# Head norms of two features in one pass of the array, roots in pairs, and the steps of a sparse-attention mixer set around them

## The reference, cut to what matters

```python
def rms_norm(x, g):
    y = xf * lax.rsqrt(jnp.mean(xf * xf, axis=-1, keepdims=True) + EPS)
...
q = rms_norm(q.reshape(B, S, DSA_HEADS, HEAD_DIM), q_g)          # 12 heads: six features of 2 heads
k = rms_norm(k, k_g)
dots = jnp.einsum('bqhd,bsd->bqhs', qib, ki) * IDX_DIM ** -0.5   # the indexer
score = jnp.einsum('bqh,bqhs->bqs', wib, jax.nn.relu(dots))
_, sel = lax.top_k(score, topk)                                  # 128 of up to 512
logits = jnp.einsum('bqhd,bqkd->bqhk', qb, k_sel) * HEAD_DIM ** -0.5 + bias
o = jnp.einsum('bqhk,bqkc->bqhc', softmax(logits), v_sel)
# beside it, with rms_norm on its queries and keys too:
xo = memory_cross_attention(xq, mk, mv, xq_g, xk_g)
```

## Time and profile before

| | |
|---|---|
| median of 3 runs | 1434.66 us (1433.44 to 1435.72) |
| the profiled execution: its own time | 1435.65 us |
| its span on the profile | 1433.8 us |
| PE busy | 1385.7 us (97%) |
| DVE busy | 591.8 us (41%) |
| ACT busy | 328.8 us (23%) |
| POOL busy | 98.2 us (7%) |
| chain that ended last | PE 69%, DMA 12%, SP's queue 8%, DVE 7%, ACT 2% |

### The profile page before, as it was taken

The page is one execution under the profiler, slowest core; times in us unless marked ns, Lnnn a source line. Parts: engine busy times, 40 slices in busy tenths (PEclk is TensorE's granted clock), DMA queues, the critical chain, the costliest instruction groups (busy, mean ns, idle before and its releaser), DMA issues.

```text
span 1433.8 us, 16567 instructions
## 1 busy us (share of the span) xinstructions
PE 1385.7 (97%) x6433; PEld 620.5 (43%) x6433; DVE 591.8 (41%) x1110; ACT 328.8 (23%) x650; POOL 98.2 (7%) x191
## 2 busy tenths in 40 slices
PE   7999999999999999999999989999999999999997
PEld 4464466433333333333354555564343333333332
DVE  4655104434333333333439974244343333333333
ACT  4455102111110110011326774221111111100111
POOL 1001000200000000000000223002000000000000
PEclk9999999999999999999999999999999999999999
DMA  8207394999999999999930030789999999999995
GB/s 284 114 0 231 105 364 174 359 422 428 426 426 427 426 426 428 427 423 421 364 101 1 1 122 1 249 337 357 422 428 426 427 427 427 426 429 424 424 421 232
DMA packets 73999, 457.26 MB, mean 319 GB/s; under 512 B 15884, under 2 KB 23628, under 8 KB 43848
## 3 DMA queue, kind: packets, MB, share of 16 engines
q1 hardware_dynamic: 68160, 447.97, 76.8%
q0 software_dynamic: 4928, 8.22, 1.5%
q10 hardware_dynamic: 840, 0.06, 0.0%
HBM read 457.41 MB, written 10.53 MB: 326 GB/s over the span
## 4 chain that ended last, share of the span: by engine, by line
PE 69%; DMA 12%; SPq 8%; DVE 7%; ACT 2%; issue 1%; POOL 0%; DVEq 0%; ACTq 0%
PE ps L1661 21%; PE ps L1274 18%; PE ps L1679 10%; DMA arena<-in_moe_w_up 8%; PE ps L1697 7%; SPq L587 5%; DMA arena<-in_moe_w_down 4%; SPq L591 3%; PE ps L1688 2%; DVE mix L1997 2%; PE ps L1650 1%; DVE small L1996 1%; PE ps L1576 1%; PE ps L1283 1%; PE ps L1535 1%
## 5 line engine op out<-in xcount | busy, mean ns | idle before, releaser
L1661 PE MATMUL ps<-arena,xT 128*64 128x512 f32 x2048 | 455.0, 596 | 14.5 <-issue 9.8
L1661 PEld LDWEIGHTS ps<-arena,xT 128*64 128x64 f32 x2048 | 150.1, 137 | 299.1 <-issue 291.9
L2335 DVE TENSOR_TENSOR x<-ps,x 128x1024 f32<-128x1024 f32 x120 | 146.5, 1224 | 204.4 <-PE ps L1697 202.1
L1679 PE MATMUL ps<-arena,xT 128*64 128x512 f32 x896 | 199.1, 596 | 2.2 <-ACT xT L1207 1.6
L1274 PE MATMUL ps<-xT,arena 128*128 128x512 f32 x384 | 169.0, 595 | 1.7 <-ACT xT L953 1.3
L1697 PE MATMUL ps<-mix,xT 128*128 128x512 bf16 x720 | 165.8, 380 | 0.0
L1697 PEld LDWEIGHTS ps<-mix,xT 128*128 128x128 bf16 x720 | 65.5, 98 | 119.5 <-issue 48.7
L1679 PEld LDWEIGHTS ps<-arena,xT 128*64 128x64 f32 x896 | 61.8, 137 | 118.4 <-issue 111.4
L1274 PEld LDWEIGHTS ps<-xT,arena 128*128 128x128 f32 x384 | 71.9, 190 | 91.4 <-issue 88.9
L1207 ACT ACTIVATE xT<-ps 128x512 f32<-128x512 f32 x32 | 19.1, 597 | 391.7 <-PE ps L1669 391.7
L1274 PE MATMUL ps<-arena,mix 128*128 128x512 f32 (+1 forms) x256 | 105.6, 568 | 0.0
(11 more groups left out here) (282 smaller groups left out, 1181.7 us busy)
## 6 DMA issues: line engine op xcount, KB each, us to landing
arena<-in_moe_w_gate SPq DMA_DIRECT2D x48, 2048.0 KB, 27.6
arena<-in_moe_w_up SPq DMA_DIRECT2D x48, 2048.0 KB, 26.4
arena<-in_moe_w_down SPq DMA_DIRECT2D x48, 2048.0 KB, 30.4
arena<-in_moe_w_down SPq DMA_DIRECT2D x32, 1024.0 KB, 20.7
arena<-in_moe_w_gate SPq DMA_DIRECT2D x32, 1024.0 KB, 21.3
arena<-in_moe_w_up SPq DMA_DIRECT2D x32, 1024.0 KB, 21.3
arena<-in_w_out SPq DMA_DIRECT2D x4, 2048.0 KB, 11.5
arena<-in_dsa_w_in SPq DMA_DIRECT2D x1, 5120.0 KB, 15.8
```

What stands on the lines that cost most here:

```text
L1661: ins = pe.matmul(ps[e * CAP:(e + 1) * CAP, bank, :], tokT[:, k, e * CAP:(e + 1) * CAP], rows_in[u][:, k, :], start=k == 0, stop=k == KD - 1)
L1679: ins = pe.matmul(ps[e * CAP:(e + 1) * CAP, BANK_Y + c, :], hT[:, j, e * CAP:(e + 1) * CAP], rows_down[u][:, j, c * 512:(c + 1) * 512], st ...
L2335: dve.tensor_tensor(x[:, t, :], ps[:, b:b + 2, :].rearrange("p a n -> p (a n)"), x[:, t, :], ALU.add).then_inc(s_, 1)
```

## The change

`norm_sum_two` takes the place of `norm_sum` for four pairs of features: `xq.0` with `xq.1` in the first mixer, `q.0` with `q.1`, `q.2` with `q.3`, `q.4` with `q.5` in the second. For each it issues four matmuls of 64 x 64 weights, one for each quarter of the array: the first feature's heads on the diagonal, the second's off it. The second feature's sums so lie in its bank with the two heads swapped (`turned`), and ACT reads that bank in two instructions of 64 partitions (`on_bank`). ACT takes Ln of both features and then Exp of both. The sums of `q.0`, `q.2` and `q.4` move behind the next feature's, the square of `q.4` behind the roots of `q.2` and `q.3`, and DVE's rounds and norms are set around them.

```diff
@@ plan(): the banks in PE's order, and who empties them @@
+            for name, last in zip(projections(), ("k", "xq.0", "xq.1")):
                 j.add(f"1.{name}", "act")
+                sums(last)
+            j.add("1.q.1", "act")
+            x_logits(0)
+            x_logits(1)
+            j.add("1.q.2", "act")
+            sums("q.0", "q.1")
...
+        turned = ["0.xq.1", "1.q.1", "1.q.3", "1.q.5"]
@@ ACT @@
+            def on_bank(dst, key, **how):
+
+                b = bank(key[0] + ".sq" + key[1:])
+                if key in turned:
+                    act.activation(dst[0:HD], b[HD:P], bias=eps[HD:P, 0:1], **how)
+                    return act.activation(dst[HD:P], b[0:HD], bias=eps[0:HD, 0:1], **how)
+                return act.activation(dst, b, bias=eps[:, 0:1], **how)
...
                     feature("q.1")
-                    roots("1.q.0")
                     x_exp(0)
                     x_exp(1)
                     feature("q.2")
-                    roots("1.q.1")
+                    root_logs("1.q.0")
+                    root_logs("1.q.1")
+                    root_exps("1.q.0")
+                    root_exps("1.q.1")
                     x_copy(0)
                     x_exp(2)
                     feature("q.3")
-                    roots("1.q.2")
                     x_copy(1)
                     x_exp(3)
                     values(0)
                     values(1)
-                    feature("q.4")
+                    raw(1, "q.4", qT[:, 4, :])
                     x_copy(2)
                     values(2)
                     values(3)
                     l_exps(0)
-                    roots("1.q.3")
+                    root_logs("1.q.2")
+                    root_logs("1.q.3")
+                    root_exps("1.q.2")
+                    root_exps("1.q.3")
+                    squares("1.q.4", qT[:, 4, :], ["1.q.4"])
                     feature("q.5")
@@ PE @@
+            def norm_sum_two(one, two):
+
+                pe.wait_ge(sq_ready, feats[two])
+                lo, hi = slice(0, HD), slice(HD, P)
+                halves = ((lo, lo, one), (hi, hi, one), (lo, hi, two), (hi, lo, two))
+                b = {key: open_bank(key[0] + ".sq" + key[1:]) for key in (one, two)}
+                for n, (r, c, key) in enumerate(halves):
+                    ins = pe.matmul(b[key][c, :], ones_head[r, r], sqb[int(key[0])][r, feats[key] % 2, :], start=True, stop=True)
+                    if n % 2:
+                        ins.then_inc(filled, 1)
...
-                            norm_sum(f"0.xq.{c}")
+                            if c == 0:
+                                norm_sum_two("0.xq.0", "0.xq.1")
...
                     project("q.1", C_Q + P)
-                    norm_sum("1.q.0")
                     x_logits(0)
                     x_logits(1)
                     project("q.2", C_Q + 2 * P)
-                    norm_sum("1.q.1")
+                    norm_sum_two("1.q.0", "1.q.1")
                     x_turn(0)
                     x_logits(2)
                     project("q.3", C_Q + 3 * P)
-                    norm_sum("1.q.2")
...
-                    norm_sum("1.q.3")
+                    norm_sum_two("1.q.2", "1.q.3")
                     project("q.5", C_Q + 5 * P)
                     x_turn(3)
                     x_value(2)
-                    norm_sum("1.q.4")
-                    norm_sum("1.q.5")
+                    norm_sum_two("1.q.4", "1.q.5")
@@ DVE @@
                     x_largest(1)
-                    normalise_q(0)
+                    take_largest(2, 10, 11)
                     x_inverse(0)
-                    take_largest(2, 10, 11)
+                    take_largest(2, 11, 12)
                     x_inverse(1)
-                    take_largest(2, 11, 16)
+                    take_largest(2, 12, 16)
                     x_copy(0)
                     x_largest(2)
+                    normalise_q(0)
                     normalise_q(1)
-                    take_largest(3, 0, 1)
                     x_inverse(2)
-                    take_largest(3, 1, 5)
+                    take_largest(3, 0, 5)
                     x_copy(1)
                     x_largest(3)
                     x_out(0)
-                    normalise_q(2)
+                    take_largest(3, 5, 6)
                     x_inverse(3)
-                    take_largest(3, 5, 9)
+                    take_largest(3, 6, 9)
...
+                    normalise_q(2)
                     normalise_q(3)
```

More of the change, by code:

```diff
@@ L224, in plan, with sums @@
             j.add("1.vT", "act")
-            last = "k"
-            for name in projections():
+            def sums(*names):
+                for name in names:
+                    j.add(f"1.sq.{name}", "act")
+            for name, last in zip(projections(), ("k", "xq.0", "xq.1")):
                 j.add(f"1.{name}", "act")
[L228 to L251, removed]
+                sums(last)
[4 more added lines that the diff above has]
+            sums("q.0", "q.1")
+            x_turn(0)
+            x_logits(2)
+            j.add("1.q.3", "act")
+            x_turn(1)
+            x_logits(3)
+            j.add("1.xo.0", "dve")
+            values(0)
+            values(1)
+            j.add("1.q.4", "act")
+            x_turn(2)
+            j.add("1.xo.1", "dve")
+            logits(0)
+            values(2)
+            values(3)
+            sums("q.2", "q.3")
+            j.add("1.q.5", "act")
+            x_turn(3)
+            j.add("1.xo.2", "dve")
+            sums("q.4", "q.5")
             logits(1)
@@ L910, in root_logs @@
                     act.wait_ge(feat_normed, n - 2)
-                act.activation(rs_view(key), bank(jn), ACT.Ln, bias=eps[:, 0:1], scale=1.0 / HD).then_inc(emptied["act"], 1)
+                on_bank(rs_view(key), key, func=ACT.Ln, scale=1.0 / HD).then_inc(emptied["act"], 1)
             def root_exps(key):
@@ L926, in roots @@
                         act.wait_ge(feat_normed, n - 2)
-                    act.activation(rs_view(key), bank(jn), ACT.Sqrt, bias=eps[:, 0:1], scale=1.0 / HD).then_inc(emptied["act"], 1)
+                    on_bank(rs_view(key), key, func=ACT.Sqrt, scale=1.0 / HD).then_inc(emptied["act"], 1)
             for L in range(2):
```

## The result

| | before | after |
|---|---|---|
| median, us (lowest to highest, 13 runs each) | 1434.66 (1431.44 to 1436.15) | 1436.74 (1435.62 to 1440.19) |
| the profiled execution: own time, span | 1435.65, 1433.8 | 1436.13, 1434.3 |
| PE, DVE, ACT busy, us | 1385.7, 591.8, 328.8 | 1381.5, 591.9, 326.1 |

The ratio of the times is 1.0021 [1.0013, 1.0029]: the change costs 2.1 us by the medians, 3.0 us by the means. The forecast was 1436.6. PE is busy 4.2 us less and the program takes longer. It fell three times in the profile before and twice in this one; e9, the kernel after once more, has four falls and PE busy for 1384.0 us, 2.5 us more. Ratios leave out three executions far from all others: one of e12 (3722.64 us) and two of the kernel before beside the experiments (5122.54 and 1469.49 us).

A forecast was written before the change was run, and what follows sets the result against it. PE and DVE were taken to run side by side, with DVE late at `q.4` and ACT taking over from `q.5`'s sums. 1434.66 + 1.1 (chain) + 0.7 + 0.2 (clock) = 1436.6 us; range 1432.5 to 1438.6.

The forecast's parts named there:

- The price of a double sum: On PE, all four quarters overlap: 0.86 us, or 1.04 us with two changes of shape.
- The third rival: Quarters of a double sum don't overlap: 1437.4 us with corners only, about 1441 us with none; chance 0.07.
- The 3.44 us: Time of a double sum on PE if no quarters overlap, as the prediction read the skill's page.
- The first mixer: PE saves 0.68 us but waits for DVE's norm of `memK`: 0.00 us gained, wait from 2.0 to 2.7 us.
- `q.4`: Second mixer: DVE stands 0.8 us for an Exp, so `q.4` starts 0.28 us later and PE waits 2.0 us.
- The saving passes through: Rival: DVE is in time, ACT's third Ln is covered, PE's -1.9 us reaches the end; 1432.8 us, chance 0.17.
- ACT to `l_exps(1)`: Second mixer: ACT runs without gaps, with half reads and three Ln; `l_exps(1)` comes 1.1 us later.
- PE's last saving hidden behind ACT: Second mixer, sums of `q.4` and `q.5`: PE's -0.78 us is hidden because ACT sets the pace.
- The clock: After the new 2.0 us wait ahead of `q.4`, the granted clock falls in 2/5 of cases: 0.7 us.
- The second rival: The clock falls every time, after the new `q.4` wait and the longer first-mixer wait; 1438.5 us, chance 0.16.
- The first mixer's clock: The longer PE wait in the first mixer can raise its own share of clock falls: 0.2 us.

The follow-up runs named there:

- e9: The kernel after once more, unaltered, timed beside e10, e11 and e12; ratio to before 1.0024.
- e12: e8 without the two extra matmuls in the first mixer; 1432.47 us beside 1434.45 for the kernel before, ratio 0.9991.
- e3: The kernel after with one DVE selection round put between the two norms and `x_inverse(2)`; ratio to before 1.0018.
- e4: The kernel after with one DVE round of the third block moved from ahead of `x_copy(1)` to behind the first group's reciprocal; ratio to before 1.0015.
- e2: The kernel after with each swapped bank read by ACT in one instruction, heads left swapped (wrong roots); ratio to before 1.0008.
- e1: The kernel after with its order kept but the second mixer's sums made singly, without packing; ratio to before 1.0020.
- e8: The kernel after with the e3 and e4 moves, single sums for `xq`, `q.4`, `q.5`, and two extra matmuls in the first mixer; 1432.39 us, ratio to before 0.9988.
- e11: The kernel after with only two repeated matmuls filling PE's first-mixer wait, ahead of `gate.0`; ratio to before 1.0013.
- e6: The kernel after with repeated matmuls filling two PE waits: two in the first mixer, three ahead of `q.4`; ratio to before 1.0008.
- e5: The kernel before with only the first mixer's sums of `xq.0` and `xq.1` packed; ratio to before 1.0003.
- e7: The kernel before with only two repeated matmuls filling PE's first-mixer wait, ahead of `gate.0`; ratio to before 0.9991.
- e10: The kernel after with only three repeated matmuls filling PE's wait ahead of `q.4`; ratio to before 1.0019.

## Why the prediction was right, step by step

The time, the range and the sign held: 1436.74 for 1436.6. ACT's stretch came out 0.5 us dearer than forecast and the fall at `q.4`, priced at 0.7, wasn't seen; that the total is met to 0.1 us is luck.

- **The price of a double sum.** Right: 1.02 us for 1.04. All four quarters start within 0.04 us of each other, and their second records 0.5 us later, in step as the corners of the block gates do. The third rival is dead. The Trainium skill ("TensorEngine Tiling (Array Packing)", Restrictions and Gotchas) says that different row tiles cannot access one PSUM bank simultaneously; the trace disagrees: both row halves write each of the two banks, and start within 0.04 us. The 3.44 us that the prediction drew from this sentence doesn't follow from it, since it says nothing of products in different banks.
- **The first mixer.** `x_logits(0)` unmoved behind a longer wait: right; the wait is 2.49 us, not 2.7. What it does to the clock is below.
- **`q.4`.** Right in mechanism and nearly in size: DVE stood 0.86 us (0.8), `q.4` came 0.36 us later (0.28), PE waited 2.13 us (2.0). e3 and e4 show the place: a round moved there moves `q.4` and all behind it. "The saving passes through" is dead with it: PE's saving became a wait.
- **ACT to `l_exps(1)`.** Right in mechanism, too small: +1.58 for +1.1, inside the bounds of -1.2 to +1.9. The term was mis-sized in two parts: the copy of `q.5` is 0.95 us late for 0.7, and the stretch behind it 6.50 us long for 5.87, +0.63 for +0.4. I had priced a half read at 0.60 from copies; as Ln it takes 0.68, and the three Ln of a pair 2.10 us (835.60 to 837.70) for 1.9. e2 shows the price of the half reads by themselves: 1.21 us.
- **PE's last saving hidden behind ACT.** Right, and it is worse than nothing: it appears as the wait of 2.27 us in the loop, which e1, e8 and e12 (single last sums) have at 0.85 to 0.88.
- **The clock.** This step failed in its place. The waits ahead of `q.4` that nothing filled (2.13, 2.11, 2.12 in e11, 1.96 and 1.60 us) were followed by 1.00 in five profiles of five; 2/5 x 1.68 = 0.7 us was a share taken from waits at other places. The fall came in the loop instead (842 to 852 us), in after, e1, e3, e4, e6, e8, e9 and e12 but not in before, e2, e5, e7, e10 and e11. It is not bound to the long wait: e8 and e12 have it behind 0.88 us, e10 and e11 don't behind 2.3. It costs some 0.5 us there. The second rival, a fall every time at `q.4` and in the first mixer, is wrong in place, and the time stayed under its 1438.5.
- **The first mixer's clock.** The forecast put 0.2 us on a fall that would come oftener behind the longer wait. The profiles don't show that it does: unfilled, the wait of 2.0 us has a fall in two profiles of two (before, e12), the one of 2.5 us in five of eight. Filled, it has none in four of four (e6, e7, e8, e11). But the fall may only have moved: e6, e8 and e11 have one at about 235 and one at about 590 us, as unfilled e4 has, and none of the seven profiles with a fall at 117 us has either. From the start of `x_logits(0)` in the first mixer to that of `x_largest(0)` in the second it takes 671.78 (after) and 672.16 us (e9) unfilled, 671.95 (e6) and 671.66 (e11) filled, so there the filling gained half a us at most.
- **The excess.** It is +1.1 us on average for the eight kernels with the packed first sum and no filling, -0.4 for the two with both (e6, e11), -1.0 for the two filled ones without packing (e7, e8), and -0.1 for before and e12. One place doesn't explain this: +1.1 for packing and -1.3 for filling the kernel before (e7) are more than one fall of 1.7 us. e5, the packing alone, has +0.4 and settles nothing.

The sum by what was measured: +1.58 at `l_exps(1)` and +0.5 for the loop's fall make +2.1 at PE's restart, which is the rise of the medians. The means rise by 0.9 us more.

The record has one more number for this, the mean granted clock of every execution. Every fall in the 14 profiles, wherever it is, takes 1.7 us of full-speed work, 0.0012 of the mean, and the profiles bear it out: 0.999 with no fall (e7), 0.997 with two (after, e2, e3), 0.994 or 0.995 with four. Over 11 executions e9, the kernel after, has 0.9942 and the kernel before beside it 0.9963: 1.7 falls more in each execution. Among the executions of one kernel, 0.0012 less of the mean clock goes with 0.9 us more (245 executions, standard error 0.1). That makes 1.6 us, an estimate; with the +1.58 of the chain it is 3.2 of the 3.3 us by which the mean of e9 is above before. The forecast had 0.9 us for the clock, the second rival 2.7. e11 has 0.7 falls fewer than e9, e10 none fewer, e5 0.3 more than before. So the price of the clock was too small, and it seems to lie in more falls, of which the loop has the clearest share; why there are more, and where the others lie, stays open. The same estimate comes within 0.9 us of all kernels whose first mixer is unfilled, but puts those with the first mixer filled (e6, e7, e8, e11) 0.7 to 1.4 us too high: their filling gains something that the number of falls doesn't explain.

Two executions of 13 took 1440 us, of which the 13 of before have none; e9 and e10 had two of 11 each, e11 two at 1439, e1 one at 1439, e2 one at 1441. Eight of these ten have a lower mean clock than their kernel's average. No profile caught one; their cause stays open.

## What to carry to other kernels

Before an engine's work is shortened, ask of each place who releases what comes next: here PE's saving of 3.2 us met DVE at `q.4` and ACT at `l_exps(1)`, and both had become later by the reordering that made the saving possible. A packed result that has to be read in two halves costs the reader a whole instruction for each half; pack where the reader has idle time, or lay the operands out so that it comes in place. Of an order written by hand, a wait that a round of other work would fill is the cheapest gain (e3, e4, e8), and a wait of the busiest engine that can't be shortened may be worth filling, if the clock then doesn't fall elsewhere.

## What the runs showed of the hardware that was not expected

- Four float32 matmuls of 64 x 64 weights by 512 columns on the four quarters take 1.02 us together, change of shape included, and start within 0.04 us, though each of the two banks is written from both row halves.
- Ln on 64 partitions takes 0.68 us, on 128 partitions 0.69.
- A fall of the granted clock to 0.50 took 1.7 us of PE's full-speed work each time, some 40 times in 14 profiles. The 16 records of `x_logits(0)` took 1.68 us more; in the loop, where PE waits for others, the path lost 0.3 to 0.6 us. The trace of e9 has two falls in the loop within 8 us (844 to 852), with the same restart to 0.06 us.
- Matmuls that compute nothing new, put into a wait of 2.0 to 2.5 us, kept the clock at 1.00 behind it in four profiles of four, where seven of ten without them had a fall; in three of the four it fell at 235 and 590 us instead.
